# VectorE's output scaling at the head of the next step in the dilated blocks of a two-block model

## The reference

```
s = einsum('bdhnqe,bdhnke->bdhnqk', qb, kb) / sqrt(E)      # scores, own and previous band
s = where(mask, s + bias, -1e30)
m = max(s);  p = exp(s - m);  den = sum(p)
o = einsum('bdhnqk,bdhnke->bdhnqe', p, vb) / den           # the scaling that this change moves
lse = m + log(den)
```

## Time and profile before

| | |
|---|---|
| runs before | 3647.24, 3650.72, 3651.54 us; median 3650.72 us |
| the profiled execution | 3652.57 us, its span 3650.8 us |
| TensorE busy | 3336.9 us, 91% of the span |
| VectorE busy | 2105.9 us, 58% |
| ScalarE, GpSimd busy | 1306.3 us and 1290.4 us, 36% and 35% |
| mean granted clock of TensorE | 0.955 |
| the dilated steps | from 2352 to 2512 us of the span |

### The profile page before, as it was taken

How to read it: one execution, slowest core, us unless ns; L and a number is a source line. 1 busy time by engine, 2 the same in 40 slices (tenths; PEclk the granted TensorE clock), 3 DMA queues, 4 the chain that set the end, 5 groups by cost and what they waited for, 6 DMA issues and landing times. The chain is left out here.

```text
span 3650.8 us, 43830 instructions
## 1 busy us (share of the span) xinstructions
PE 3336.9 (91%) x16295; PEld 2663.9 (73%) x16295; DVE 2105.9 (58%) x3004; ACT 1306.3 (36%) x2270; POOL 1290.4 (35%) x1028
## 2 busy tenths in 40 slices
PE   5699999989899999969999999588889989999998
PEld 3577777776688888747888888375557768888887
DVE  5346664465876767883333333575555465555586
ACT  3523333143433334432223333153652233322344
POOL 4121212112655530145544454260435235544111
PEclk8799999889999999979999999799999999999999
DMA  8621112123233347224555332751025523333552
GB/s 255 221 61 46 51 57 90 49 99 110 70 116 101 101 140 241 75 70 134 115 113 121 116 116 93 203 164 64 31 67 152 167 93 101 98 104 101 199 183 98
DMA packets 357916, 418.46 MB, mean 115 GB/s; under 512 B 29798, under 2 KB 257586, under 8 KB 356282
## 3 DMA queue, kind: packets, MB, share of 16 engines
q1 hardware_dynamic: 350968, 391.84, 34.9%
q0 software_dynamic: 6016, 16.93, 1.9%
q10 hardware_dynamic: 722, 6.89, 0.5%
HBM read 294.06 MB, written 120.88 MB: 114 GB/s over the span
## 5 line engine op out<-in xcount | busy, mean ns | idle before, releaser
L2348 POOL TENSOR_TENSOR up_w_lo<-up_w_sum,up_w_hi 128x512 fp32r<-128x512 f32 x176 | 248.5, 1440 | 326.4 <-ACT up_w_hi L2324 324.5
L3282 POOL TENSOR_TENSOR px_w_lo<-px_w_sum,px_w_hi 128x512 fp32r<-128x512 f32 x140 | 204.8, 1493 | 281.4 <-ACT px_w_hi L3133 281.4
L2348 POOL TENSOR_TENSOR up_w_lo<-up_raw,up_w_hi 128x512 fp32r<-128x512 f32 x132 | 201.4, 1541 | 127.5 <-ACT up_w_hi L2324 127.5
L1924 ACT CAST down_hi<-down_room 128x1024 fp32r<-128x1024 f32 x154 | 161.0, 1051 | 210.7 <-PE ps L2204 137.1
L1928 DVE TENSOR_TENSOR down_lo<-down_room,down_hi 128x1024 fp32r<-128x1024 f32 x154 | 190.0, 1239 | 72.6 <-ACT down_hi L1924 71.4
L2324 ACT CAST up_w_hi<-up_w_sum 128x512 fp32r<-128x512 f32 x176 | 99.7, 614 | 323.5 <-DVE up_w_sum L2337 323.5
L766 PE MATMUL ps<-h_hi,stream_hi 128*128 128x512 f32 (+1 forms) x488 | 184.7, 378 | 24.5 <-POOL stream_lo L741 17.2
L2554 PE MATMUL ps<-h_hi_at,up_w_lo 128*128 128x512 f32 x704 | 191.3, 394 | 15.7 <-POOL up_w_lo L2348 15.7
L2554 PE MATMUL ps<-h_hi_at,up_w_hi 128*128 128x512 f32 x704 | 192.5, 396 | 8.0 <-ACT up_w_hi L2324 8.0
L3133 ACT CAST px_w_hi<-px_w_sum 128x512 fp32r<-128x512 f32 x140 | 79.9, 617 | 310.8 <-DVE px_w_sum L3213 310.8
L2554 PE MATMUL ps<-h_lo_at,up_w_hi 128*128 128x512 f32 x704 | 189.3, 391 | 0.0
(11 more groups left out here) (607 smaller groups left out, 8138.0 us busy)
## 6 DMA issues: line engine op xcount, KB each, us to landing
up_raw<-in_w_up SPq DMA_DIRECT2D x88, 512.0 KB, 4.2
down_room<-hid_kept SPq DMA_DIRECT2D x154, 256.0 KB, 2.9
hid_kept<-up_out SPq DMA_DIRECT2D x44, 512.0 KB, 3.6
down_room<-in_w_down SPq DMA_DIRECT2D x88, 256.0 KB, 4.3
px_raw<-in_w_in SPq DMA_DIRECT2D x38, 512.0 KB, 5.2
proj_kept<-xT SPq DMA_DIRECT2D x34, 512.0 KB, 6.0
px_raw<-in_w_gate SPq DMA_DIRECT2D x32, 512.0 KB, 5.2
gates_kept<-xT SPq DMA_DIRECT2D x32, 512.0 KB, 5.2
```

The costliest lines, as they stand in the source:

```text
L1924: nc.scalar.copy(hi[:, u % R], both(u)).then_inc(hi_made, 1)
L2348: nc.gpsimd.tensor_tensor(w_lo[:, s, :], source(t, i), w_hi[:, s, :].bitcast(F32), ALU.subtract).then_inc(lo_made, 1)
L3282: nc.gpsimd.tensor_tensor(self.w_lo[:, s, :], self.source(t, i), self.w_hi[:, s, :].bitcast(F32), ALU.subtract).then_inc(self.lo_made, 1)
```

## The change

VectorE scales the output of a block at the head of the next step. In step j it now begins with `output(j - 4)`, where it ended its own part of the step with `output(j - 3)`. What each instruction computes, and on which engine, stays as it is. Nothing changes on the other engines' queues.

```
         for j in range(N_DIL):
+            if 0 <= j - 4 < BLOCKS:
+                output(j - 4)
             if j < BLOCKS:
                 largest(j)
             if 0 <= j - 2 < BLOCKS:
                 take_turned(j - 2)
-            if 0 <= j - 3 < BLOCKS:
-                output(j - 3)
             if j >= 11 and (j - 11) % NB == 0:
                 log_sums((j - 11) // NB)
             yield
```

## The result

The changed kernel took 3666.97 us (median of 5 runs, 3663.66 to 3668.76), the kernel before 3650.72 us (5 runs). The ratio is 1.0045, with a 95% interval of 1.003 to 1.006: 16 us slower, where 4.3 us were forecast.

The account below looks back on a forecast made before the run. The prediction took TensorE to bound the kernel. Its delays, 2.11 us before pass 1 and 2.15 us in the gates' part, summed to 4.26 us, so 3650.72 + 4.3 = 3655.0 us, with a range of 3649.5 to 3660.5 us.

Parts of the forecast that it names:

- The bound: TensorE, busy for 91% of the span; an edit on VectorE was to count only where TensorE waits for it.
- the steps named: Steps 4, 7, 11, 22 and 25, where TensorE's value product was to wait for a scaling behind other VectorE work.
- The sum: 2.11 us up to pass 1 plus 2.15 us in the gates' part, 4.26 us slower in all.
- Step 4 ... +1.33 us: Block 0's scaling, now behind scan 1 on VectorE, was to start TensorE's value product 1.33 us later.
- I add nothing for these steps: Steps 8 to 15: later products were to be covered by GpSimd's states and 3.71 us idle before pass 3.
- +2.15 us in all: Step 25: block 21's scaling behind the second gate multiply delays the product by 2.15 us, including step 22's 0.57.
- The clock: Rival: 2.2 us idle in step 11 drops pass 2 to TensorE's lower clock; 3658.8 us, chance 0.14.
- The price, 3.8 us: Extra time forecast for pass 2 at the lower clock, from pass 3's 9.2 us against pass 1's 5.4 us.
- The idle time that gives some delay back: TensorE's 0.97 us wait for a DMA at 2406.66, counted as giving about 1 us of delay back.
- absorbed: Rival: slack hidden in TensorE's full stretch shrinks the 2.11 us before pass 1 toward nothing; 3652.9 us, chance 0.13.
- freed case: Rival: VectorE, freed of scaling waits such as step 24's 1.03 us, makes the kernel faster; 3649.7 us, chance 0.07.

Follow-up runs that it names:

- the two filled kernels: Unneeded transposes in TensorE's idle times: in the changed kernel's longer waits, ratio 1.0005; in the kernel before, before pass 2, pass 3 and first gate product, 0.9988.
- block 0 alone: Only the scaling of block 0 moved, behind scan 1 in step 4, against the kernel before: ratio 1.001 (1.0001 to 1.0018).

## Why the prediction was wrong

- *The bound and the steps named were right.* TensorE waited for L3580 in steps 4, 7, 11, 22 and 25, for 1.19, 1.07, 1.82, 0.45 and 1.50 us (forecast about 1.3, 0.8, 2.2, 0.6 and 1.6). One wait more, 0.39 us in step 15, was harmless, as it lies ahead of the idle time before pass 3.
- *The sum was right as a sum of waits.* With the clock held up, the change cost 194.51 - 190.05 = 4.46 us in the stretch; 4.26 were forecast. The ratios of the two filled kernels, 1.0005 and 0.9988, are some 6 us apart, which agrees within their intervals.
- *The step that failed* was the sum's silent premise that the work behind a wait runs as fast as before. "Step 4 ... +1.33 us" was 3.6 us with block 0 alone. "I add nothing for these steps" was 4.06 us from pass 2 to pass 3. "+2.15 us in all" behind the first gate product was 6.20 us, 3.4 us of it in the two slower products of step 25. The table's 16.35 us less the 4.46 us of waits leaves 11.9 us, three quarters of the loss, for the clock. The kernel before pays 4.3 us for it already (194.39 - 190.05), at pass 3 and the first gate product.
- *The clock was a rival, but sized wrongly.* It had pass 2 alone, with a chance of 0.14. The argument against it, that 1.40 us of idle time before pass 2 did not bring the clock down, rested on one execution. With the order of instructions unchanged up to step 24, the kernel that moves only block 21 ran pass 2 in 7.74 us behind the same GpSimd wait. The other, the 1.80 us before the gate product at 2513.94, held: that product took 7.13 us in all thirteen traces. The price, 3.8 us, was nearly right: a pass took 9.03 to 9.07 us wholly at the lower clock and 4.94 to 5.02 us at the full one (the 9.2 us in the prediction is the busy time of a window that ran on behind the pass). The step 4 wait was never asked the same question, though it is a wait in a stretch that had none.
- *The idle time that gives some delay back* was counted as a gain alone. The DMA's 0.97 us did go, but then 2.29 to 2.60 us stood before pass 2 in the three kernels with a late pass 1 and no wait in step 11, and pass 2 took 8.28 to 9.06 us there. So the delay of pass 1 and the wait of step 11 can each bring pass 2 down, and in some executions the 1.4 us of the order before do.
- *The absorbed and the freed case* did not happen. VectorE's multiply in step 24 waited for its sigmoid as before, and the loss reached pass 1 in full.
- *The range* (to 3660.5 us) left out 3667 us because the clock was given only one place.

The intervals of the two measurements of the change, 11 to 22 us and 7 to 15 us, overlap. The table rests on one trace of the kernel before. Its pass 2 took 5.02 us, and 7.48 and 7.74 us in two kernels with no delay ahead of it; a trace of the kernel before with the longer form would have put the loss in the stretch at some 13 to 14 us (an estimate from these numbers). How often its timed runs have which form isn't shown, since they have no traces.

## What to carry to other kernels

Where TensorE is saturated, price a new wait twice: with its length, and with the half rate of the microseconds of work behind it. Ask this of every new wait, even of 1 to 2 us. A scaling that frees a PSUM bank should stand ahead of unrelated work in its engine's queue. Where idle time can't be removed, a few unneeded transposes into a free bank in it can be worth more than they cost.

## What the runs showed of the hardware

Idle times of 1 to 2 us on TensorE do not all have the same effect. Waits of 1.19 or 1.20 us in step 4 (4 of 4 traces), of 1.8 to 2.1 us in step 11 (3 of 3) and of 1.50 us in step 25 (3 of 3) were followed by the lower clock. Waits of 1.07 to 1.13 us in step 7 (0 of 3) and of 0.45 us in step 22 (0 of 3) were not, nor were 1.79 or 1.80 us before the gate product of sixteen matmuls (7.13 us in 13 of 13). So the length of the idle time doesn't decide alone. The 1.4 us before pass 2 were followed by it in two of three traces that had no delay ahead of them, the 2.3 to 2.6 us that a late pass 1 left there in three of three, and the 3.7 to 5.6 us before pass 3 in ten of ten. Why step 7 and the gate product are spared and step 4 is not stays open; the work before a wait may count as well. The half rate held for most or all of 9 us in pass 2, and cost 2.2 to 2.3 us behind the wait of step 4 in all four traces.
